# Squared lengths of q and k as eight rows from 512-token products, behind the decay sums

## The reference, cut to what matters

```python
def _l2norm(x):
    xf = x.astype(jnp.float32)
    return xf * lax.rsqrt(jnp.sum(xf * xf, axis=-1, keepdims=True) + EPS)
...
g = -exp(a_log) * softplus(a + dt_bias)          # per token and head
gcum = jnp.cumsum(gc, axis=-1)                   # within a chunk
decay = jnp.where(incl, jnp.exp(jnp.where(incl, diff, 0.0)), 0.0)
a_kk = jnp.where(strict, jnp.einsum('bnhcd,bnhsd->bnhcs', k_beta, kc) * decay, 0.0)
t_mat = a_kk + jnp.eye(CHUNK)                    # then a triangular solve
```

## Time and profile before

| | us |
|---|---|
| median of 3 runs | 3759.94 (3759.68 to 3762.35) |
| the profiled execution's own time | 3770.26 |
| its span, first to last instruction | 3768.7 |
| mean granted TensorE clock over the span | 0.899 |
| TensorE busy | 3130.4 (83%) |
| VectorE busy | 893.7 (24%) |
| ScalarE busy | 507.2 (13%) |

### The profile page before, as it was taken

One profiled execution on the slowest core, in us unless ns is written; L12 is line 12 of the kernel. 1 busy time (PEld: TensorE's weight loads), 2 busy tenths in 40 slices (PEclk: granted clock), 3 DMA queues, 4 the chain that ended last, 5 costly groups with the idle time before them and its releaser, 6 DMA issues.

```text
span 3768.7 us, 36964 instructions
## 1 busy us (share of the span) xinstructions
PE 3130.4 (83%) x15390; PEld 1402.6 (37%) x15390; DVE 893.7 (24%) x1287; ACT 507.2 (13%) x967; POOL 238.9 (6%) x342
## 2 busy tenths in 40 slices
PE   7988845558899998999866589999699732999998
PEld 3475534323232333333333444444333211444443
DVE  2233232241111111111132331001331391120013
ACT  1020121000000000000011230000200580100001
POOL 0000001020111011111000000000100130000000
PEclk8989956769999999999987799999899866999999
DMA  7109810176999999999750031221121003032110
GB/s 251 39 20 367 331 21 10 45 302 250 402 392 404 402 404 400 399 400 401 313 219 0 0 117 45 89 89 61 57 63 55 20 6 95 12 139 89 67 67 23
DMA packets 167091, 646.67 MB, mean 172 GB/s; under 512 B 20091, under 2 KB 29883, under 8 KB 126337
## 3 DMA queue, kind: packets, MB, share of 16 engines
q1 hardware_dynamic: 150562, 603.81, 41.9%
q0 software_dynamic: 14528, 37.56, 3.3%
q10 hardware_dynamic: 1856, 3.21, 0.3%
HBM read 630.68 MB, written 18.38 MB: 172 GB/s over the span
## 4 chain that ended last, share of the span: by engine, by line
PE 41%; issue 28%; DVE 5%; DMA 3%; POOL 3%; POOLq 2%; ACT 1%; DVEq 1%; ACTq 0%; PEldq 0%
PE ps L2080 12%; PE ps L2091 12%; PE ps L2208 6%; PE ps L2384 3%; PE ps L1899 2%; DMA stage<-gate_dram 2%; PE ps L1022 2%; PE ps L2030 1%; POOLq L1408 1%; PE ps L1921 1%; POOL work L1417 1%; PE ps L1933 1%; DVE slots L2353 1%; PE ps L1738 0%; DVE small L1973 0%
## 5 line engine op out<-in xcount | busy, mean ns | idle before, releaser
L1516 PE MATMUL ps<-slots,hT 128*32 128x512 f32 x5120 | 581.1, 599 | 18.6 <-DMA slots<-in_w_up_dram 7.9
L2080 PE MATMUL ps<-hT,slots 128*128 128x512 f32 x1024 | 448.5, 599 | 13.1 <-issue 6.6
L2091 PE MATMUL ps<-slots,work 128*128 128x512 f32 x1024 | 441.8, 593 | 12.2 <-DVE work L2128 12.2
L1516 PEld LDWEIGHTS ps<-slots,hT 128*32 128x32 f32 x5120 | 160.1, 110 | 414.8 <-issue 399.0
L2080 PEld LDWEIGHTS ps<-hT,slots 128*128 128x128 f32 x1024 | 195.1, 192 | 265.7 <-issue 265.7
L2091 PEld LDWEIGHTS ps<-slots,work 128*128 128x128 f32 x1024 | 193.7, 190 | 258.8 <-issue 247.5
L1552 PE MATMUL ps<-slots,work 128*32 128x512 f32 x2112 | 253.6, 607 | 26.6 <-DMA slots<-in_w_down_dram 17.0
L2208 PE MATMUL ps<-hT,slots 128*96 128x512 f32 x512 | 223.4, 597 | 26.4 <-DVEq L2214 24.6
L2384 PE MATMUL ps<-slots,work 96*128 96x512 f32 x256 | 112.5, 601 | 107.4 <-DVE work L2371 107.4
L1667 DVE TENSOR_SCALAR stage<-ps 128x512 f32<-128x512 f32 (+1 forms) x47 | 32.2, 686 | 581.7 <-PE ps L1518 581.3
L1552 PEld LDWEIGHTS ps<-slots,work 128*32 128x32 f32 x2112 | 88.7, 111 | 158.9 <-issue 126.0
(11 more groups left out here) (539 smaller groups left out, 3049.3 us busy)
## 6 DMA issues: line engine op xcount, KB each, us to landing
slots<-in_w_up_dram SPq DMA_DIRECT2D x128, 2048.0 KB, 19.3
slots<-in_w_down_dram SPq DMA_DIRECT2D x64, 2048.0 KB, 17.4
slots<-in_mlp_w_dram SPq DMA_DIRECT2D x32, 2048.0 KB, 9.0
slots<-in_ada_w_dram SPq DMA_DIRECT2D x16, 2048.0 KB, 9.8
slots<-in_w_ada_dram SPq DMA_DIRECT2D x12, 2048.0 KB, 8.6
slots<-in_ada_w_dram SPq DMA_DIRECT2D x16, 1024.0 KB, 6.9
slots<-in_rnn_w_in_dram SPq DMA_DIRECT2D x8, 1536.0 KB, 6.9
slots<-in_w_in_dram SPq DMA_DIRECT2D x5, 2048.0 KB, 17.6
```

Of the source, the lines that this page charges most:

```text
L1516: ins = pe.matmul(to, x[:, k, unit * UNIT:(unit + 1) * UNIT], upw[s][:, k % 2, col:col + CH], start=k == 0, stop=False)
L2080: ins = pe.matmul(ps[:, m], slots[:, s, k, m * P:(m + 1) * P], hT[:, k, :], start=k == 0, stop=k == KT - 1)
L2091: ins = pe.matmul(ps[:, 4 + 2 * (t % 2) + h], h1T[:, k, t * P:(t + 1) * P], slots[:, 2 + h, k], start=k == 0, stop=k == KT - 1)
```

## The change

Three things are moved or replaced. First, TensorE makes the decay sums (L582, L583) directly behind `products(0)`, ahead of the squared lengths and of `products(1)`. Second, the squared lengths are made by eight products over all 512 tokens. The stationary operand is 128 by 8, all zeros but for one column of ones at place `j` (a slice of a 15-column constant that the mask transfer now brings along), and the squared row moves; the eight products add up in rows 0 to 7 of bank 7. VectorE copies these eight rows to `sqrow` in `stage`. After `sums(0)` TensorE turns them with four products (8 by 128 stationary, 8 columns of the identity moving), and VectorE makes `rqk` and `arow` from the result in `lengths()`, between `sums(0)` and `sums(1)`. Third, ScalarE's Sqrt for `rroot` moves from behind the Ln to the head loop, at `h == 2`, ahead of `turned_system(2)`.

```diff
-            for j in (4, 5, 6, 7, 0, 1, 2, 3):
-                pe.wait_ge(S("sq_ready"), (j + 4) % 8 + 1)
-                for u in range(TT):
-                    ins = pe.matmul(ps[:, 7, 4 * j + u:4 * j + u + 1], sqs[:, j, u * P:(u + 1) * P], ones[:, 0:1], start=True, stop=True)
-            ins.then_inc(S("dn_scalar_pe"), 1)
-            products(1)
             pe.wait_ge(S("dn_scalar_dve"), DN_STEP["g_ready"])
             pe.matmul(ps[:, 4, 64:80], upper[:], g_, start=True, stop=True)
             pe.matmul(ps[:, 4, 80:96], lowstrict[:], g_, start=True, stop=True).then_inc(S("dn_scalar_pe"), 1)
+            pe.wait_ge(S("dn_in"), 48)
+            for n, j in enumerate((4, 5, 6, 7, 0, 1, 2, 3)):
+                pe.wait_ge(S("sq_ready"), n + 1)
+                ins = pe.matmul(ps[0:8, 7], one_at[:, 7 - j:15 - j], sqs[:, j], start=n == 0, stop=n == 7)
+            ins.then_inc(S("dn_scalar_pe"), 1)
+            products(1)
             sums(0)
+            pe.wait_ge(S("dn_scalar_dve"), DN_STEP["sq_row"])
+            for u in range(TT):
+                ins = pe.matmul(ps[:, 7, u * 8:(u + 1) * 8], sqrow[:, u * P:(u + 1) * P], ident[0:8, 0:8], start=True, stop=True)
+            ins.then_inc(S("dn_scalar_pe"), 1)
             sums(1)
...
-            a.wait_ge(S("dn_scalar_dve"), DN_STEP["rr_ready"])
-            a.activation(rroot, rqk, ACT.Sqrt).then_inc(S("dn_scalar_act"), 1)
...
                 if h + 1 < DH:
                     exps(h + 1)
+                if h == DH - 2:
+                    a.wait_ge(S("dn_scalar_dve"), DN_STEP["rr_ready"])
+                    a.activation(rroot, rqk, ACT.Sqrt).then_inc(S("dn_scalar_act"), 1)
                 turned_system(h)
...
-            v.wait_ge(S("dn_scalar_pe"), DN_STEP["sq_sum"])
-            v.tensor_scalar(rqk[:, 0:16], ps[:, 7, 0:16], EPS, float(DD), ALU.add, ALU.mult)
-            v.tensor_scalar(rqk[:, 16:32], ps[:, 7, 16:32], EPS, None, ALU.add)
-            v.drain()
-            v.reciprocal(rqk, rqk).then_inc(S("dn_scalar_dve"), 1)
             v.wait_ge(S("dn_scalar_act"), DN_STEP["sp_ln"])
...
-            v.wait_ge(S("dn_scalar_act"), DN_STEP["beta_ready"])
-            v.scalar_tensor_tensor(arow, beta, -1.0, rqk[:, 16:32], ALU.mult, ALU.mult)
             v.wait_ge(S("dn_scalar_pe"), DN_STEP["gcum_ps"])
             v.tensor_copy(gcol, ps[:, 4, 64:80])
             v.tensor_scalar(ngcol, ps[:, 4, 64:80], -1.0, None, ALU.mult).then_inc(S("dn_scalar_dve"), 1)
+            v.wait_ge(S("dn_scalar_pe"), DN_STEP["sq_sum"])
+            v.tensor_copy(sqrow, ps[0:8, 7]).then_inc(S("dn_scalar_dve"), 1)
+
+            def lengths():
+                v.wait_ge(S("dn_scalar_pe"), DN_STEP["sq_turned"])
+                lens = ps[:, 7, 0:32].rearrange("p (u j) -> p j u", j=8)
+                v.tensor_scalar(by_pair(rqk[:, 0:16]), lens[:, 0:4], EPS, float(DD), ALU.add, ALU.mult)
+                v.tensor_scalar(by_pair(rqk[:, 16:32]), lens[:, 4:8], EPS, None, ALU.add)
+                v.drain()
+                v.reciprocal(rqk, rqk).then_inc(S("dn_scalar_dve"), 1)
+                v.drain()
+                v.scalar_tensor_tensor(arow, beta, -1.0, rqk[:, 16:32], ALU.mult, ALU.mult)
+                v.drain()
...
             sums(0)
+            v.wait_ge(S("dn_scalar_act"), DN_STEP["ek_ready"])
+            lengths()
```

More of the change, by code:

```diff
@@ L68, in constants @@
     k["dnmask"] = np.concatenate([np.where(low, 0.0, -NEG), np.where(same & ~low, 0.0, NEG), band(1), np.eye(P) + band(1).T]
-                                 + [band(2 << i) for i in range(5)], axis=1).astype(np.float32)
+                                 + [band(2 << i) for i in range(5)]
+                                 + [np.broadcast_to(np.arange(15)[None, :] == 7, (P, 15))], axis=1).astype(np.float32)
     kj = np.arange(2 * P)[None, :]
@@ L508, in build @@
         dmask = scratch0[:, 14336:14336 + 9 * P].rearrange("p (m n) -> p m n", m=9)
+        one_at = scratch0[:, 14336 + 9 * P:14336 + 9 * P + 15]
+        sqrow = stage[0:8, CH:2 * CH]
         flatH = hT[:].rearrange("p k t -> p (k t)")
@@ L522, in build @@
         o_ss, o_sc = small[:, 0:16], small[:, 16:32]
-        DN_STEP = {"beta_ready": 1, "sp_ln": 2, "root_ready": 3, "ek_ready": 4, "ab_ready": 1, "rr_ready": 2, "g_ready": 3, "gcol_out": 4, "scalars": 5, "sq_sum": 1, "gcum_ps": 2}
+        DN_STEP = {"beta_ready": 1, "sp_ln": 2, "ek_ready": 3, "root_ready": 4, "ab_ready": 1, "g_ready": 2, "gcol_out": 3, "sq_row": 4, "rr_ready": 5, "scalars": 6, "gcum_ps": 1, "sq_sum": 2, "sq_turned": 3}
         NLEV = 5
@@ L545, in dn_moves @@
             sp.memset(edge[:, 1:TT], 0.0)
-            sp.dma_start(scratch0[:, 14336:14336 + 9 * P], A["k_dnmask"]).then_inc(S("dn_in"), 16)
+            sp.dma_start(scratch0[:, 14336:14336 + 9 * P + 15], A["k_dnmask"]).then_inc(S("dn_in"), 16)
         def dn_pe(pe):
@@ L807, in dn_dve @@
                 v.tensor_tensor(invT[:, h], sysT[:, h], rows4(3), ALU.mult).then_inc(S("inv_begun"), 1)
-            v.wait_ge(S("dn_scalar_act"), DN_STEP["ek_ready"])
             v.wait_ge(S("dn_scalar_act"), DN_STEP["root_ready"])
```

## The result

| comparison, each with its own runs of the kernel before | median, us | ratio to before, 95% interval |
|---|---|---|
| first (11 runs each) | 3774.41 against 3764.02 | 1.0024 [1.0015, 1.0034] |
| second (11 and 35 runs) | 3766.53 against 3762.98 | 1.0012 [1.0003, 1.0021] |
| third (11 and 29 runs) | 3771.62 against 3765.90 | 1.0014 [1.0005, 1.0023] |

The change makes the kernel slower. 3774.4 us, the first comparison, lies outside the range of 3754 to 3769 and 12.5 us above the predicted 3761.9. Of these, 4.1 us lie in the starting point: the prediction was carried over to 3759.94, the median of 3 runs of the kernel before, and 11 runs have 3764.02. The forecast difference of +2.0 us is a ratio of 1.0005. The first comparison excludes it clearly; it lies inside the interval of the second and on the lower end of the third.

A forecast was written before the change was run, and what follows sets the result against it. TensorE's old lengths, then VectorE's heads, were taken to set the weight stream's first load. Terms of +0.4, +0.1 and +1.4 us and the clock gave +2.0 there; from 3759.94 that made 3761.9 us, range 3754 to 3769.

The forecast's parts named there:

- L578 takes 13.65 us: TensorE's old squared lengths: 64 instructions from 230.38 on, with products(1), the decay sums and sums(0) queued behind.
- -4.45 us: TensorE's new products of the lengths, 9.2 us, against 13.65 for the old; bounds -5.9, -4.0, or +0.15 if the clock stays low.
- -0.85 us: sums(0) on TensorE and its hand-over to VectorE: 1.13 us at clock 1.00 instead of 1.98.
- The start of the lengths, +8.0: On TensorE the lengths wait behind the decay sums and start at 238.4 instead of 230.38; nothing hides this.
- The products of the lengths, 9.2 us: TensorE's 16 new instructions: 4.6 us at clock 0.50, then 4.6 us for the other 10.7 instructions.
- Rival 1: The narrow products of the lengths don't raise TensorE's clock: +7.9 us, 3768 us; chance 0.10.
- Turning the rows: nothing: The copy to sqrow, four turning products and VectorE's lengths() lie under other work, with 0.7 us of slack: 0.
- The Sqrt, +1.4: In ScalarE's head loop, table load of 1.28 us and Sqrt of 0.1 delay head 2's copy, on the path; bounds 0 and 1.5.
- Rival 3: The table switch costs its drain too, so the Sqrt holds ScalarE 1.4 us longer: 3763.3 us; chance 0.05.
- To the first load, "+2.0 us": SP's first load of the weight stream is issued 1.4 to 3.3 us later, +2.0 taken; the stream passes it on whole.
- Rival 2: TensorE's clock is up early and stays through the last turn and first weight piece: faster, 3757.5 us; chance 0.15.
- The stage ends with this stream: The weight stream ends the stage, so the change is worth the shift of SP's first load.

The follow-up runs named there:

- second trace of before: The kernel before, nothing changed, profiled again and timed against itself: ratio 1.0003.
- mask run: The kernel before with only the mask constant made 15 columns wider and loaded with them: ratio 0.9989.
- run with the Sqrt alone: The kernel before with only the Sqrt moved, from behind the Ln to ahead of the copy of head 2's turned system: ratio 1.0005.
- order alone: The kernel before, its 64 narrow products kept, with the decay sums ahead of them, VectorE's lengths behind those sums and the Sqrt behind the head loop: ratio 1.0034.

## Why the prediction was wrong

- **The step that failed** is the cost of the old lengths, L578. The prediction has "L578 takes 13.65 us" and "It stands at 0.50 here" of the clock. Both are true of the profiled execution, one trace in four: the other three of the old order have 10.86, 10.54 and 10.76 us. In those the new products replace 10.7 us, so "-4.45 us" should have been -1.5. With it the sum at VectorE's first sum is +3.3 (8.0 - 1.5 - 1.6 - 0.72 - 0.85); measured, 24.0 (253.62 - 229.63) against 20.2 us in the second trace of before: +3.8. In the mask run and the run with the Sqrt alone the old order's first sum starts earlier still, at 19.0 and 18.7 us: the clock rose once more before their `sums(0)`, so that "-0.85 us" is nothing there and the change costs 5.0 to 5.3. No rival had it, for I asked whether the clock would rise in the new products, never whether it sometimes rises in time for the old ones.
- **This step is not the whole miss.** It turns the forecast of +2.0 us at SP's first load into +5.0. Measured, the changed kernel's three traces have it at 54.72 us of the stage in the mean and the three traces with a short L578 at 48.56: +6.2. The forecast with +5.0 would still have been 3765 us. Of the 12.5 us between 3774.4 and 3761.9, 4.1 are the starting point and 8.4 the difference (10.4 instead of 2.0). L578 is 3.0 of these and the other local terms 1.2. The last 4.2 lie behind the first load or in chance between comparisons: the mean of the three ratios gives 6.3 us, not 10.4.
- **The start of the lengths, +8.0: right.** The decay sums start 10.9 us after the stage's start (240.49 - 229.63), as the 237.7 - 226.8 of the prediction; the lengths at 11.8, 0.2 us later than forecast.
- **The products of the lengths, 9.2 us: right,** 9.05 to 9.29 in the three traces. The clock rose 4.1 to 4.6 us in. The 4.6 was a choice between two rows, so that it fits this well is in part luck. Rival 1 fell: behind an operand 8 columns wide the clock rose. "Turning the rows: nothing" was right too: VectorE's L815 of head 0 waited for ScalarE (0.92 us), not for the lengths.
- **The Sqrt, +1.4: right for the wait,** 1.29 us in the changed kernel and in the one with the Sqrt alone. What it didn't see is that a slow turn of head 2's system costs about as much at the same place without the Sqrt (1.34 and 1.18 us). Rival 3 fell with it: the Sqrt starts 0.01 us after its load ends, and the copy starts 0.14 us behind that, so the total of 2.66 us that the Trainium skill gives for a switch (ScalarE: Activation LUTs, section What ACT_TABLE_LOAD costs) is not what this place pays.
- **To the first load, "+2.0 us": undersized** even against the profile that it was worked out from: +3.5 (54.8 against 51.3 us of the stage), 0.2 over its bound. The clock was 0.50 from before the last turn until after it (273.4 to 281.3), so all 16 instructions ran at 0.50 (3.7 us against 2.6), and `turn_system(0)` cost 0.45, not 0.1. Compared with the second trace of before it is +6.6.
- **Rival 2** (the clock is up early and stays) is in its first half (the clock is up early) what the old order with wide products does, not what the change does.
- **"The stage ends with this stream": not to the end.** SP's last single loads are 5.8, 6.9, 5.8, 7.9 and 5.8 us apart in all fourteen traces, and in all of them TensorE has no idleness from the first of these loads to the next weights (the output weights): there its own work sets the pace, not the transfers. Before, then the changed kernel:

```profile
421.20:459.40 38.20, 38.20 (x313) 25.71 (x314) 10.85 (x26) 9.15 (x34) 0.00 (x0) 1.00 0.89 320
429.10:467.30 38.20, 38.20 (x313) 25.71 (x314) 10.84 (x26) 7.76 (x33) 0.00 (x0) 1.00 0.87 320
```

- **What stays open:** of the 7.7 us between the stages' mean lengths, 5.3 stand at the first load and 2.4 behind it. From this load to the meeting it is 190.5 to 194.7 us in all kernels; the changed kernel's three have 193.5 to 194.7, the four of the old order with narrow products 190.7 to 193.2, and the others lie over the whole range. Most of the difference is made in the 17 loads that start 34 us behind the first (95.4 to 100.9 us), up to 1.6 in one round of 10.2 us instead of 8.6. In the changed kernel's first trace, the only one of its three with that long round, the clock fell to 0.50 in it. Whether the 2.4 us belong to the change isn't shown. The first comparison gave 1.0024, the later two 1.0012 and 1.0014; their intervals overlap, and whether more than chance lies between them isn't settled.

## What to carry to other kernels

A queue that waits cost twice on TensorE here: the time, and the clock that it would have had, or did have, without the wait. Before a reorder is priced against one profiled execution, ask of every dense stretch ahead of the replaced work whether the clock may have risen behind it in another one, and profile the kernel before twice. A cheaper form and a new order should be tried apart: here the form gains and the order loses more. Two delays that end at the same wait, as the Sqrt and a slow turn do here, must not be added.

## What the runs showed of the hardware

The same kernel's stage was 243.8 and 238.8 us long in two executions; 3.1 us of this (51.3 against 48.2 at the first load) come from the clock at its start. Products with an 8-column stationary operand and 512 moving columns were followed by a clock of 1.00 after 4.1 to 4.6 us, and run at 0.44 us an instruction at 1.00 (7.03 / 16), as fast as those of 128 columns (23.34 / 54 = 0.43). Eight instructions of filler at 1.00 did not keep the clock over the 4 us of idleness behind them; with sixteen, which left no gap, it stayed at 1.00. With the order alone it stood at 1.00 for 2.9 us of idleness (234.9 to 237.8) and was 0.50 in the same idleness from 238.9 on. It also fell while TensorE was busy without a gap, in the 64 narrow instructions of L578 (234.2 to 241.6 in the second trace of before).
